# A hybrid attention layer on one core: top-k rounds placed one per unit, gate stores issued when their chunk ends, gate loads spread

## The reference

```python
mod = einsum('bd,de->be', silu(c), w_ada) + b_ada
shift, scale, gate = split(mod, 3, axis=-1)
proj = einsum('btd,de->bte', rmsnorm(x, ln_gain) * (1 + scale) + shift, w_in)
# group A: latent attention. group B: indexer scores, top-k keys, softmax over these with a bias
score = einsum('btgs,btg->bts', relu(dots), w_idx)
top_val, sel = lax.top_k(score, min(256, S // 4))
y = concat([rmsnorm(o_a) * silu(g_a), rmsnorm(o_b) * silu(g_b)])
out = x + gate * einsum('bte,ed->btd', y, w_out)      # then a last rmsnorm
```

## Time and profile before

| what | value |
|---|---|
| median of three runs | 986.52 us |
| the profiled execution: its own time, its span | 986.52 us, 984.7 us |
| PE busy, share of the span | 930.2 us, 94% |
| DVE busy | 425.3 us, 43% |
| ACT busy | 341.2 us, 35% |
| POOL busy | 119.0 us, 12% |
| chain that ended last | PE 87%; DMA 3%; ACT 3%; DVE 3%; SPq 2%; issue 1% |
| mean DMA rate | 188 GB/s |

### The profile page before, as it was taken

How to read it: one execution, slowest core, us unless ns; L and a number is a source line. 1 busy time by engine, 2 the same in 40 slices (tenths; PEclk the granted TensorE clock), 3 DMA queues, 4 the chain that set the end, 5 groups by cost and what they waited for, 6 DMA issues and landing times.

```text
span 984.7 us, 14197 instructions
## 1 busy us (share of the span) xinstructions
PE 930.2 (94%) x5707; PEld 795.3 (81%) x5707; DVE 425.3 (43%) x882; ACT 341.2 (35%) x629; POOL 119.0 (12%) x189
## 2 busy tenths in 40 slices
PE   2798799999999999999999999999999999999996
PEld 0366478899998688888999988888888989788885
DVE  1222343336432144433332463237645556596462
ACT  2312342333321334223331352223243344663351
POOL 1000003101200000011111300002001112741000
PEclk9999989999999999999999999999999999999998
DMA  8999958665543224355333767536866763695423
GB/s 317 387 330 363 346 186 259 165 149 159 150 128 97 65 86 140 114 178 181 101 100 108 233 216 255 188 102 170 264 220 212 234 223 106 205 312 161 129 65 128
DMA packets 129537, 185.37 MB, mean 188 GB/s; under 512 B 30048, under 2 KB 79896, under 8 KB 128320
## 3 DMA queue, kind: packets, MB, share of 16 engines
q1 hardware_dynamic: 115744, 138.71, 44.6%
q0 software_dynamic: 13728, 45.76, 14.2%
HBM read 173.84 MB, written 12.69 MB: 189 GB/s over the span
## 4 chain that ended last, share of the span: by engine, by line
PE 87%; DMA 3%; ACT 3%; DVE 3%; SPq 2%; issue 1%; DVEq 0%; ACTq 0%
PE proj L1738 32%; PE proj L1727 29%; PE proj L1754 2%; SPq L694 2%; PE bankO L1711 2%; DMA raw<-in_w_in 2%; DMA araw<-in_w_ada 2%; PE proj L1711 2%; PE bankO L1835 1%; PE bankO L1844 1%; PE bankS L1754 1%; PE bankS L1727 1%; PE bankS L1961 1%; DVE w_lo L1278 1%; PE bankT L1976 1%
## 5 line engine op out<-in xcount | busy, mean ns | idle before, releaser
L1278 DVE TENSOR_TENSOR w_lo<-raw,w_hi 128x1024 fp32r<-128x1024 f32 (+2 forms) x164 | 197.8, 1208 | 238.7 <-ACT w_hi L940 238.0
L940 ACT ACTIVATE w_hi<-raw 128x1024 fp32r<-128x1024 f32 (+2 forms) x164 | 167.8, 1026 | 187.0 <-PE proj L1727 102.7
L1738 PE MATMUL proj<-hT_hi,w_hi 128*128 128x384 f32 x640 | 222.7, 348 | 1.9 <-ACT misc L940 1.1
L1738 PE MATMUL proj<-hT_hi,w_lo 128*128 128x384 f32 x640 | 214.6, 335 | 0.0
L1738 PE MATMUL proj<-hT_lo,w_hi 128*128 128x384 f32 x640 | 214.3, 335 | 0.0
L1727 PE MATMUL proj<-w_hi,hT_hi 128*128 128x512 f32 (+2 forms) x464 | 180.9, 390 | 10.2 <-DVE w_lo L1278 8.2
L1727 PE MATMUL proj<-w_hi,hT_lo 128*128 128x512 f32 (+2 forms) x464 | 176.0, 379 | 0.0
L1727 PE MATMUL proj<-w_lo,hT_hi 128*128 128x512 f32 (+2 forms) x464 | 175.9, 379 | 0.0
L1738 PEld LDWEIGHTS proj<-hT_hi,w_hi 128*128 128x128 f32 x640 | 120.2, 188 | 14.2 <-issue 11.7
L1738 PEld LDWEIGHTS proj<-hT_lo,w_hi 128*128 128x128 f32 x640 | 120.3, 188 | 0.5 <-issue 0.2
L1738 PEld LDWEIGHTS proj<-hT_hi,w_lo 128*128 128x128 f32 x640 | 120.1, 188 | 0.0
(11 more groups left out here) (350 smaller groups left out, 1035.5 us busy)
## 6 DMA issues: line engine op xcount, KB each, us to landing
raw<-in_w_in SPq DMA_DIRECT2D x104, 512.0 KB, 3.7
araw<-in_w_ada SPq DMA_DIRECT2D x128, 256.0 KB, 7.1
raw<-in_w_ada SPq DMA_DIRECT2D x32, 512.0 KB, 4.6
raw<-in_w_out SPq DMA_DIRECT2D x32, 512.0 KB, 3.9
raw<-in_w_in SPq DMA_DIRECT2D x32, 256.0 KB, 3.2
raw<-in_w_in SPq DMA_DIRECT2D x32, 128.0 KB, 2.5
wuk<-in_w_uk POOLq DMA_DIRECT2D x16, 256.0 KB, 3.7
kload<-in_cache_dsa_k POOLq DMA_DIRECT2D x8, 512.0 KB, 5.7
```

The lines of the kernel that those rows point to most:

```text
L940: return nc.scalar.activation(out, in_, func, scale=scale, **kw)
L1278: V.tensor_tensor(w_lo[:, SLOT[u], 0:w], raw_of(u)[:, 0:w], high(u)[:, 0:w].bitcast(F32), ALU.subtract).then_inc(lo_ready, 1)
L1738: ins = mm(banks[blk][:, 0:TOK], w[:, n, cols], a[:, kt, :], start=first and n == m == 0, stop=final and n == per - 1 and m == 2)
```

## The change

The eight `tk` steps stand behind units 191 to 198, one each, and no longer behind every other unit up to 205. `ld_mask` moves from unit 206 to 196, `comb` from 209 to 198. The step `st_gate` is gone; its code runs on POOL at the last unit of each gate chunk (183 and 215), ahead of the steps planned there. `ld_g` 8 to 15 no longer stand all behind unit 234: `max(u, v - 3)` puts 8 to 11 there, 12 and 13 behind unit 235, and 14 and 15 behind unit 236. No instruction is added or removed.

```diff
-    run(u, "tk", len(ROUNDS), 2)
-    put(u + 2 * len(ROUNDS) - 1, ("ld_mask", 0))
-    put(u + 2 * len(ROUNDS) + 2, ("comb", 0))
+    for n in range(len(ROUNDS)):
+        put(u + n, ("tk", n))
+    put(u + 5, ("ld_mask", 0))
+    put(u + 7, ("comb", 0))
...
-    put(u + 3, ("st_gate", 0), ("st_gate", 1))
...
         v = max(u + 2 + i // 2, LAST_UNIT["gb", i // 2] + (6 if i >= 6 else 2))
-        put(u, ("ld_g", 8 + i))
+        put(max(u, v - 3), ("ld_g", 8 + i))
         put(v, ("y", 8 + i))
...
-        def st_gate(j):
-
-            moved(pool, "gate", j)
-            for g in range(4):
-                c0 = 1024 * j + 256 * g
-                pool.dma_start(gate_d[:, c0:c0 + 256], modA[32 * g:32 * g + 9, j, :]).then_inc(gate_out, 16)
...
+            if last_unit(u) and kind == "gate":
+                moved(pool, kind, j)
+                for g in range(4):
+                    c0 = 1024 * j + 256 * g
+                    pool.dma_start(gate_d[:, c0:c0 + 256], modA[32 * g:32 * g + 9, j, :]).then_inc(gate_out, 16)
             for name, n in PLAN[u]:
                 if name in steps:
                     steps[name](n)
```

More of the change, by code:

```diff
@@ L903, in _ @@
                                          ld_uk, ld_krc, ld_ck, ld_cn,
-                                         ld_kic, ld_g, ld_k, ld_v, ld_kc, ld_vc, yh, st_gate, ld_res, ld_gate, ld_fgain)}
+                                         ld_kic, ld_g, ld_k, ld_v, ld_kc, ld_vc, yh, ld_res, ld_gate, ld_fgain)}
         for u, (c, k) in enumerate(UNITS):
```

## The result

The changed kernel took 1005.23 us (median of four runs, 1002.33 to 1007.56), the kernel before beside it 987.49 us: ratio 1.0175, 95% interval 1.015 to 1.02. It is slower by 17.7 us, where +12.7 with a range up to 1004.0 had been forecast. The direction was right, the size was too small, and the time lies outside the range.

A forecast was written before the change was run, and what follows sets the result against it. The prediction took PE, busy 94% of the span, to bound the kernel. Three added PE waits, 4.0 + 3.3 + 5.4 = 12.7 us on 986.5, gave 999.2 us, with a range from 992.0 to 1004.0.

The forecast's parts named there:

- What bounds the kernel: PE, busy 94% of the span; only what makes PE stand, or lets it stand less, counts.
- Part 1: Top-k rounds one a unit: DVE's work pressed into units 191 to 198 makes PE wait for unit 202's split, +4.0 us.
- The single waits: PE's growing lateness at bank O (1.5 us), the split of unit 200 (2.6) and that of unit 202 (4.0).
- Rival (b): DVE's lateness is mostly absorbed because splits run ahead of PE; only the other two moves cost: 995.2 us, chance 0.08.
- Part 2: Gate 1's stores on POOL at unit 215 delay ld_kc 1, so PE waits for keys in ks 1: +3.3 us.
- the landing: Time from the issue of ld_kc 1 to its keys being there: 4.9 us, range 4.0 to 6.5.
- Part 3: Group B's later gate loads hold up ACT and POOL, so PE waits ahead of unit 242: +5.4 us.
- Block 14: Gate load gl_b 14, queued on POOL behind gateB and fgain; to land at 886.3 us, between 884.6 and 887.9.
- Rival (a): The late gl_b loads pass or share with the big ones and land in time: 993.8 us, chance 0.16.
- Sum: Three waits on PE's path add, 4.0 + 3.3 + 5.4 = 12.7 us, giving 999.2 us; chance 0.60.
- Rival (c): Held at silu 14, ACT delays the splits of units 243 and 244; PE waits again: about 1005 us, chance 0.08.
- Rival (d): Not slower: the new order removes PE waits between 733 and 857 us, at best -4.75: 982 to 986, chance 0.08.

The follow-up runs named there:

- l1_gl_first: The changed kernel with ld_gate and ld_fgain one unit later, so gl_b 14 and 15 are issued ahead of them; 996.74 us, ratio 1.0094 to the kernel before.
- p3_gl: The kernel before with only the later gate loads 12 to 15 of group B; 995.57 us, ratio 1.0086.
- g1_kc_first: The changed kernel with the gate stores behind the steps of their unit, gate 1's thus behind ld_kc 1; 999.31 us, ratio 1.0113 to the kernel before.
- d2_two_stores: The kernel before with the gate stores moved to units 183 and 215, two of four ahead of the unit's steps, two behind; 988.97 us, ratio 1.002.
- p1_tk: The kernel before with only the tk steps one a unit and ld_mask and comb earlier; 990.36 us, ratio 1.0041.
- f1_fill_ks: The changed kernel with 24 useless products on PE in the wait for the keys of ks 1; 1002.86 us, ratio 1.0163 to the kernel before.
- f2_fill_both: The changed kernel with useless products in both long PE waits, 24 in ks 1 and 30 ahead of unit 242; 1002.34 us, ratio 1.0149 to the kernel before.
- h2_tk_mended: The changed kernel with gate 1's stores behind ld_kc 1 and gl_b 12 to 15 ahead of gateB and fgain; 990.65 us, ratio 1.0041 to the kernel before.

## Why the prediction was wrong

**What bounds the kernel** held: PE had no wait to lose in these stretches, and everything late in a queue beside it came out as time.

**Part 1** was forecast at +4.0; the stretch grew by 4.2 in the profile and the part alone cost 4.0 (0.41%). The single waits, forecast as 1.5, 1.1 more and 1.4 more, were 1.43, 1.04 and 1.24; from product start to product start each is some 0.15 longer, which makes the 4.2. Rival (b) fails.

**Part 2** was forecast at +3.3; the wait was 4.1. The stores, their place and the issue of `ld_kc` 1 came out as worked out: forecast 739.3, and 747.96 - 8.35 = 739.6 in the trace (unit 215 started 8.35 later than before). The term that was mis-sized is the landing: 4.9 taken from the nearest row, 5.3 measured, and 3.7 to 5.7 over the experiments (5.7 in l1_gl_first); the issue 0.3 later is the rest. That `ld_kc` 2 and the values stay hidden held.

**Part 3** was forecast at +5.4; the wait was 4.84 and 4.96 in the two profiles of the changed kernel (5.0 and 5.1 from start to start), 5.45 in p3_gl. Block 14 was forecast to land at 886.3, and landed near 901.5, less the 15.1 by which the kernel was late there: 886.4. To hit it to 0.1 us is in part luck, since the forecast took the middle between two bounds 3.3 apart. From the landing to unit 242 it was 4.3 us, not the 4.8 of the sum. Rival (a), that late small loads pass the large ones, fails. The order of landing in POOL's queue held in l1_gl_first too.

**Sum.** This is the step that failed: "The three waits stand one after another on PE's path, and each moves all that follows, so they add". The waits do add (4.2 + 4.1 + 5.0 = 13.3, with the fillers 13.7 for the whole kernel). But the sentence takes each wait at its own length, with PE's work behind it at the speed of before. The work behind the two long waits ran at the lower clock: 2.0 to 2.8 us more behind `ks` 1, and 1.5 to 2.5 for the first 36 products behind unit 242's wait; 4.4 and 3.5 in all in the two profiles of the changed kernel. The sum had this at nothing, without a reason. Against its 12.7, the 17.7 are 0.2 more for part 1, 0.8 more for the wait of part 2, 0.4 less for that of part 3, and 4.4 for the clock. The prediction read that the clock was 1.00 in its three windows and did not ask what a PE that stands would do to it. The kernel before has no wait over 1.4 us after 640 us. But its first stage has, and its trace held a warning. Two waits there have the same length and the same products behind them; the timeline of PE at both, and the windows around the second and behind the first:

```profile
79.26 0.50 PE L1727 MATMUL proj<-w_hi,hT_hi 128*128 128x512 f32 x1 [2.71 <-DVE w_lo L1278]
...
107.81 0.50 PE L1727 MATMUL proj<-w_hi,hT_hi 128*128 128x512 f32 x1 [2.71 <-DVE w_lo L1278]
```

```profile
80.00:82.00 2.00, 2.00 (x10) 1.64 (x10) 0.14 (x1) 0.00 (x0) 0.00 (x0) 1.00 1.08 372
82.00:84.00 2.00, 2.00 (x16) 1.30 (x18) 0.00 (x0) 0.00 (x0) 0.00 (x0) 1.00 1.06 387
...
106.00:108.00 2.00, 0.19 (x1) 0.19 (x2) 1.47 (x2) 0.98 (x2) 0.00 (x0) 1.00 1.05 398
108.00:110.00 2.00, 2.00 (x7) 1.58 (x7) 0.69 (x2) 0.00 (x0) 0.00 (x0) 0.66 1.05 391
110.00:112.00 2.00, 2.00 (x7) 1.51 (x6) 0.00 (x0) 0.00 (x0) 0.00 (x0) 0.50 1.08 366
112.00:114.00 2.00, 2.00 (x16) 1.33 (x18) 0.00 (x0) 0.00 (x0) 0.00 (x0) 0.99 1.06 384
```

PE stood 2.71 us each time. Behind the first wait the clock stayed at 1.00, and 18 products started within 3.98 us (79.26 to 83.24); behind the second it was at the lower level for some 3.4 us, and the same 18 took 5.60 us (107.81 to 113.41): 1.6 us more. These rows say that the clock can fall behind a wait of this length, not that it must. Put at 1.6 us for each of the two long waits, they would have given 999.2 + 3.2 = 1002.4, and a range moved by as much would have held the result. The 4.4 us that the falls cost in the profile are more than that.

Rival (c) named a time of about 1005, that is close to the measured one, by a mechanism that did not occur: PE had no second wait ahead of unit 243. Rival (d) fails: no wait between 733 and 857 us went away, and `ld_kc` 1 took 3.7 us or more to land in every trace in which it stood at unit 215 behind stores.

## What to carry to other kernels

Where one engine is busy without a gap, a change of order in the queues beside it can win nothing there and can cost, and what it costs is found by asking, for each moved step, what stands behind it on its engine and when that is wanted. When a wait is added on PE, price it twice: the time that it stands, and the work behind it at the lower clock, which here came to between 0.3 and 0.7 of a wait of 4 to 5.5 us; look for it in another stage of the same trace if the stage at hand has no such wait. If the wait can't be removed, something for PE to do in it keeps the clock up, though it brings the data no sooner, and what it gained in time here was within the noise.

## What was not expected of the hardware

The clock fell in or just behind every wait of PE of about 4 us or more after 640 us (ten of them, 3.97 to 5.45 us, in eight profiles), and never where fillers took the place of the wait. Behind waits of 1.43 us it fell twice (g1_kc_first, d2_two_stores) and stayed at 1.00 in seven others of the same length (both profiles of the changed kernel, p1_tk, f1_fill_ks, f2_fill_both, l1_gl_first, h2_tk_mended), as it did behind one of two waits of 2.71 us in one trace. What tells these apart stays open, and so does what a fall costs, 1.5 to 2.8 us. The key load of `ld_kc` 1 (512 KB) landed 5.0 to 5.7 us after its issue with four small gate stores just ahead of it, 3.7 with two and 3.8 with eight of half the size. The number of stores doesn't order these times, and their cause was not pursued.
